# Remainders of perceptron weights made by adding transfers instead of VectorE

## The reference, cut to what matters

```python
def sq_relu_mlp(h, w_up, w_down):
    u = jax.nn.relu(h @ w_up)
    return (u * u) @ w_down
```

## Time and profile before

| what | value |
|---|---|
| runs | 1935.07, 1935.68, 1937.64 us |
| span of the profiled execution, which is also its own time as far as the profile shows | 1937.4 us |
| TensorE busy (share of the span) | 1912.2 us (99%) |
| VectorE busy | 1333.0 us (69%) |
| ScalarE busy | 837.4 us (43%) |
| GpSimd busy | 121.1 us (6%) |
| DMA | 182.62 MB, mean 94 GB/s |
| granted TensorE clock, mean | 0.998 |

### The profile page before, as it was taken

One profiled execution on the slowest core, in us unless ns is written; L12 is line 12 of the kernel. 1 busy time (PEld: TensorE's weight loads), 2 busy tenths in 40 slices (PEclk: granted clock), 3 DMA queues, 4 the chain that ended last, 5 costly groups with the idle time before them and its releaser, 6 DMA issues.

```text
span 1937.4 us, 32713 instructions
## 1 busy us (share of the span) xinstructions
PE 1912.2 (99%) x14002; PEld 1646.6 (85%) x14002; DVE 1333.0 (69%) x1755; ACT 837.4 (43%) x1254; POOL 121.1 (6%) x130
## 2 busy tenths in 40 slices
PE   8999999999999999999999999999999999999998
PEld 6877898888788898887989889889987788898897
DVE  5576869576677777767545687767677768777665
ACT  4333744344354344344224443434444645344342
POOL 1055100000000000010000000000002300000000
PEclk9999999999999999999999999999999999999999
DMA  8221402237123233224220233323342113233231
GB/s 271 88 66 66 137 10 80 88 132 128 46 89 108 87 110 109 88 78 140 90 87 23 66 98 98 109 87 109 102 144 88 50 47 106 90 106 109 87 109 44
DMA packets 138831, 182.62 MB, mean 94 GB/s; under 512 B 4917, under 2 KB 103429, under 8 KB 138304
## 3 DMA queue, kind: packets, MB, share of 16 engines
q1 hardware_dynamic: 135392, 168.91, 26.9%
q0 software_dynamic: 3296, 11.63, 2.9%
HBM read 172.66 MB, written 7.34 MB: 93 GB/s over the span
## 4 chain that ended last, share of the span: by engine, by line
PE 94%; DVE 3%; ACT 1%; issue 1%; DMA 0%; SPq 0%; DVEq 0%; ACTq 0%
PE X L1597 20%; PE M L1509 19%; PE M L1510 19%; PE M L1511 19%; PE X L643 3%; PE M L1570 1%; PE M L1571 1%; PE M L1572 1%; PE M L1925 1%; PE X L1902 1%; PE X L1913 1%; PE X L1780 1%; PE X L1749 1%; DMA raw<-in_w_in_dram 0%; PE X L1511 0%
## 5 line engine op out<-in xcount | busy, mean ns | idle before, releaser
L1510 PE MATMUL M<-u,raw_lo 128*128 128x512 f32 x728 | 287.9, 396 | 0.0
L1509 PE MATMUL M<-u,w_hi 128*128 128x512 f32 x728 | 287.9, 395 | 0.0
L1511 PE MATMUL M<-u,w_hi 128*128 128x512 f32 x728 | 286.1, 393 | 0.0
L2021 ACT ACTIVATE w_hi<-raw 128x2048 fp32r<-128x2048 f32 x113 | 215.6, 1908 | 93.5 <-PE M L1511 47.9
L2076 ACT ACTIVATE us<-X 128x256 f32<-128x256 f32 x156 | 60.2, 386 | 426.9 <-PE X L1597 426.9
L2549 DVE TENSOR_TENSOR h<-h,M 128x512 f32<-128x512 f32 x184 | 123.7, 685 | 144.7 <-PE M L1511 144.6
L1597 PE MATMUL X<-t,w_hi 128*128 128x256 f32 x936 | 173.2, 282 | 0.0
L1511 PEld LDWEIGHTS M<-u,w_hi 128*128 128x128 f32 x728 | 137.6, 189 | 32.8
L1509 PEld LDWEIGHTS M<-u,w_hi 128*128 128x128 f32 x728 | 136.8, 188 | 30.8
L1510 PEld LDWEIGHTS M<-u,raw_lo 128*128 128x128 f32 x728 | 136.7, 188 | 29.8
L2399 DVE TENSOR_TENSOR raw_lo<-raw,w_hi 128x2048 fp32r<-128x2048 f32 x57 | 130.3, 2287 | 23.7 <-ACT w_hi L2021 23.7
(11 more groups left out here) (525 smaller groups left out, 4542.2 us busy)
## 6 DMA issues: line engine op xcount, KB each, us to landing
raw<-in_w_up_dram SPq DMA_DIRECT2D x48, 1024.0 KB, 5.4
raw<-in_w_down_dram SPq DMA_DIRECT2D x48, 1024.0 KB, 5.0
raw<-in_w_in_dram SPq DMA_DIRECT2D x12, 1024.0 KB, 8.6
raw<-in_a_w_in_dram SPq DMA_DIRECT2D x12, 1024.0 KB, 5.3
h<-in_x_dram SPq DMA_DIRECT2D x16, 256.0 KB, 4.8
raw<-in_w_mk_dram SPq DMA_DIRECT2D x4, 1024.0 KB, 4.9
raw<-in_w_mv_dram SPq DMA_DIRECT2D x4, 1024.0 KB, 5.2
raw<-in_w_out_dram SPq DMA_DIRECT2D x4, 1024.0 KB, 5.1
```

The costliest lines, as they stand in the source:

```text
L1509: mm(dst, wh, xh, start=start, stop=False)
L1510: mm(dst, wl, xh, start=False, stop=False)
L1511: return mm(dst, wh, xl, start=False, stop=stop)
L2021: nc.scalar.activation(hi_of(n)[:, :, :], raw[:, n % 4], ACT.Copy).then_inc(S["w_hi_ready"], 1)
```

## The change

For the 48 down blocks and for quarters 1 to 3 of the 39 seven-product blocks, the remainder is made in two steps. ScalarE writes -hi over the raw weights (`raw_lo` <- -1.0 * `raw`, rounded to fp32r): in `hi` right behind the rounding of a down block, and in `quarters_neg` behind the fourth group of a seven-product block. Then GpSimd issues transfers with `accum_op=ALU.add` that read the same weights from DRAM again and add them to `raw_lo`, so that w - hi stands there: one transfer of 1 MB (4 rows of 2 KB in each of 128 partitions) for a down block, two for the quarters (4 rows of 512 bytes in each partition, then 4 rows of 1 KB). VectorE no longer does `lo` of down blocks nor `group_lo` 0 and 1; it goes on making the remainders of the sums. TensorE waits for all transfers of a block before its first matmul (`rest_ready`). GpSimd issues a block's transfers only when the block two earlier in this list has been taken up by TensorE: its first product, or its first finished chunk of a down block. Blocks U0 to U2 and all stages outside the perceptrons stay as they were. Some semaphores are merged to make room (`ld_tables`, `bias_step`).

```diff
@@ TensorE @@
+            def rest_ready(n):
+                wait(f"rest_lo{REST[n] % 2}", REST_DONE[n])
+
             def block_ready(n):
-                pe.wait_ge(S["w_lo_ready"], STD_NO[n] + 1)
+                if n in DOWN:
+                    rest_ready(n)
+                else:
+                    wait("w_lo_ready", LO_NO[n] + 1)
...
-                weights_ready(1)
+                rest_ready(n)
...
                 product(n, "P1", nth)
-                weights_ready(2)
                 product(n, "P2", nth)
-                weights_ready(3)
+                weights_ready(1)
...
-                weights_ready(4)
+                weights_ready(2)
@@ GpSimd: called for each perceptron @@
+            def remainders(first):
+
+                up, down = mlps[first]
+                for n in range(first, first + 32):
+                    if n not in REST:
+                        continue
+                    k, (_, _, _, g, b) = REST[n], MLP_AT[n]
+                    pool.wait_ge(S["rest_neg"], k + 1)
+                    if k >= 2:
+                        before = REST_AT[k - 2]
+                        if before in DOWN:
+                            pool.wait_ge(S["acc_done"], DONE[before] + 1)
+                        else:
+                            pool.wait_ge(S["st_mm"], 7 * FAST[before] + PRODUCT_NO["P1"])
+                    if n in DOWN:
+                        pool.dma_start(wide(raw_lo[:, n % 4]), down[:, 4 * g:4 * g + 4, 512 * b:512 * b + 512],
+                                       accum_op=ALU.add).then_inc(S[f"rest_lo{k % 2}"], 16)
+                    else:
+                        c, to_ = 512 * g + BW * b, quarters(raw_lo, n)
+                        w = up.rearrange("p (m j) n -> p m j n", j=2)
+                        pool.dma_start(to_[:, :, P:2 * P], w[:, :, 0, c + P:c + BW],
+                                       accum_op=ALU.add).then_inc(S[f"rest_lo{k % 2}"], 16)
+                        pool.dma_start(to_[:, :, BW:2 * BW], w[:, :, 1, c:c + BW],
+                                       accum_op=ALU.add).then_inc(S[f"rest_lo{k % 2}"], 16)
@@ ScalarE @@
+                if n in DOWN:
+                    nc.scalar.activation(raw_lo[:, n % 4], raw[:, n % 4], ACT.Copy, scale=-1.0).then_inc(S["rest_neg"], 1)
...
+            def quarters_neg(n):
+
+                act.wait_ge(S["st_sum"], 3 * FAST[n] + 3)
+                act.wait_ge(S["st_hi"], 4 * FAST[n] + 2)
+                x_, l_ = quarters(raw, n), quarters(raw_lo, n)
+                nc.scalar.activation(l_[:, :, P:4 * P], x_[:, :, P:4 * P], ACT.Copy, scale=-1.0).then_inc(S["rest_neg"], 1)
@@ VectorE, steady loop @@
                 for i in range(4, 30, 2):
                     add(i - 1, 3)
-                    lo(n + i + 1)
                     if i < 28:
                         sums(i + 2)
-                        group_lo(n + i + 2, 0)
-                        group_lo(n + i + 2, 1)
                     up_even(n + i)
                     up_odd(n + i)
```

More of the change, by code:

```diff
@@ L112 @@
 FAST, STD_NO, MLP_AT, HI_FREE = {}, [], {}, []
+DOWN, LO_NO, REST = {}, [], {}
 def mlp_order(last):
@@ L141 @@
                 continue
+            if _kind == "D":
+                DOWN[_n] = len(DOWN)
             _chunks = 4 if _kind == "D" else 2
@@ L156 @@
 STD_NO.append(N_END - len(FAST))
+LO_NO.append(STD_NO[-1] - len(DOWN))
+REST_AT = sorted([*DOWN, *FAST])
+REST_DONE, _count = {}, [0, 0]
+for _k, _n in enumerate(REST_AT):
+    REST[_n] = _k
+    _count[_k % 2] += 16 if _n in DOWN else 32
+    REST_DONE[_n] = _count[_k % 2]
 PRODUCTS = dict(P1=(4, 0, 3), P2=(6, 1, 0), P6=(2, 5, 3), P5=(1, 3, 2), P7=(0, 4, 3), P4=(5, 6, 1), P3=(3, 2, 2))
@@ L609, in rwkv_pe @@
                 if st == "zw":
-                    wait("ld_lora", 48)
+                    wait("ld_tables", 48)
                     wait("rw_lora", 1)
@@ L988, in gla_pe @@
             wait("acc_evac", ACC[N_GQK])
-            wait("ld_gk", 64)
+            wait("ld_tables", 160)
             wait("fold_step", 5)
@@ L1457, in _ @@
             pool.wait_ge(S["norm_ss"], 2)
[L1458 to L1461, removed]
+            pool.dma_start(onehot[:], A["onehot"]).then_inc(S["ld_tables"], 16)
+            pool.dma_start(relx[0:32, :], A["rel_table_2"]).then_inc(S["ld_tables"], 16)
+            pool.dma_start(relx[32:33, :], A["consts"][0:1, CONST["ones"][0]:CONST["ones"][0] + 16]).then_inc(S["ld_tables"], 16)
+            pool.wait_ge(S["bias_step"], 2)
             pool.dma_start(bias_rows, biasrow[:].unsqueeze(1).to_broadcast([16, P, 384])).then_inc(S["st_bias"], 16)
             pool.wait_ge(S["st_bias"], 16)
+            remainders(N_MLP1)
             for c in range(1, KT):
@@ L1606, in weights_ready @@
                 def weights_ready(k):
-                    wait("st_lo", 4 * j + k)
-                weights_ready(1)
+                    wait("st_lo", 2 * j + k)
+                rest_ready(n)
                 if j % 13 == 0:
@@ L1817, in mem_transposes @@
                 else:
-                    wait("bias_ev", 1)
+                    wait("bias_step", 2)
                 for t in range(2):
@@ L1845, in _ @@
             mem_scores(1)
-            wait("ld_rel", 48)
-            mm(X[3][0:16, 0:384], relx[:], onehot[:], start=True, stop=True).then_inc(S["bias_mm"], 1)
+            wait("ld_tables", 96)
+            mm(X[3][0:16, 0:384], relx[:], onehot[:], start=True, stop=True).then_inc(S["bias_step"], 1)
             chunk(N_MQ + 2, 1, x2_hi, x2_lo)
@@ L2619, in mlp @@
                 add(29, 3)
-                lo(n + 31)
                 final(30)
```

29 lines of the change are left out of this document (14 added, 15 removed).

## The result

The changed kernel took 1991.8 us (median of four runs, 1986.2 to 1993.9) against 1936.7 of the kernel before beside it (1935.1 to 1938.6): ratio 1.0283, 95% interval 1.0266 to 1.0299. Slower was right and the time is inside the range, but the forecast was 1957.0: it had 21 of the 55 us. The profiled execution is the quickest of the four; its span is 1984.3 us, 46.9 more than before.

A forecast was written before the change was run, and what follows sets the result against it. TensorE, busy 1912.2 of 1937.4 us, was taken as the bound; three starts 18.6, last up blocks 0.5 and tail 2.2 summed to 21.3 us, giving 1957.0 us on the median of 1935.68; range 1945 to 2050.

The forecast's parts named there:

- What bounds the kernel, and VectorE's relief at 0: Whole kernel: TensorE bounds it; it did not wait for VectorE's 4.1 us in a pair, so 0 gained.
- Rival C: Steady pairs: without VectorE's reads and writes products come closer, steps 2% shorter, 1932.6 us; chance 0.04.
- ScalarE's side in a pair at 0: Steady pairs: added negating copies of 1.90 and 1.46 us leave 3.4 us spare before the next snapshot, cost 0.
- What an adding transfer takes: All adding transfers: counted as twice the bytes, 7.7 us for a down block and 7.0 for the quarters.
- Steady pairs at 0: Steady pairs: quarters have 8.7 us for 7.0, 1.7 spare; DMA engines at 88%; cost 0.
- rival B: Steady pairs: DMA engines or transfer latency become the bound; 2088 us at three times the bytes; chance 0.28.
- Starts, 6.2 each: Start of each perceptron: TensorE stands 5.85 us for the first down block; 6.2 us each, 18.6 for three.
- rival A: All adding transfers: as quick as plain ones; starts 4.3 us each, tail nothing, 1949.1 us; chance 0.13.
- Last up block, 0.15 each: Last up block of each perceptron: a negation delays the second snapshot; 0.15 us each, 0.5 in all.
- Tail, 2.2: Kernel's end: the very last down block lands at 1908.9, first use at 1906.73; 2.2 us.
- Rival D: Starts: unseen slack and transfers landing within 2 us make no difference, 1936 us; chance 0.03.

The follow-up runs named there:

- e5: Changed kernel with the quarters negated earlier, about 4.5 us in each steady pair, same work and transfers: 1972.8 us.
- e2: Changed kernel with the quarters' remainders made by VectorE as before, only the down blocks by adding transfers: 1972.8 us.
- e8: Changed kernel, quarters negated early, VectorE making each perceptron's first two down blocks, first seven-product block and last two down blocks: 1936.0 us.
- e1: Changed kernel with transfers that overwrite instead of adding, so it computes something else: 1955.9 us.
- e7: Changed kernel with nine float32 matmuls of constants, read by nobody, ahead of the wait for each perceptron's first down block: 1980.3 us.
- e10: The changed kernel itself measured again, nothing altered: 1988.2 us, five runs from 1984.1 to 1994.2.

## Why the prediction was right or wrong, step by step

- **What bounds the kernel, and VectorE's relief at 0:** right. Pairs without a late transfer are 254.0 us for twelve with VectorE busy for 11.0 instead of 15.2 us of a pair. Rival C, that products come closer, is out: e5, e2 and e8 have the relief, or most of it, and the old step.
- **ScalarE's side in a pair at 0:** right. 1.90 and 1.48 us for the negations (1.90 and 1.46 worked out), and e5 and e8 have pairs of the old length.
- **What an adding transfer takes:** the first step that failed, and the term of the sum that was mis-sized. 7.7 us was taken for a down block, from the end of its negation to its use, and 7.0 for the quarters. At D3 it is 10.2. The runs show what the 2.5 between are. Some 0.6 is the time from the negation to the issue, which the sum put at nothing. Some 0.8 is the transfer by itself: 8.5 us from issue to landing in the tail with nothing beside it. Some 1.1 is SyncE's load, issued 1.45 us behind it: with it the landing takes 9.6. The plain part was right: 5.2 was taken, and e1's transfer in the same rows takes 5.3 alone and 5.4 in the median beside SyncE's loads. It was the adding that was priced too low: 2.5 us were taken, the price of a plain MB in rows of 8 KB, and it costs 3.1 alone and 4.1 in the median (5.4 to 9.5). Doubling the bytes was right as to the part of a row that goes with them (38 to 76 ns for a KB), but 8-KB rows were the wrong row to take it from: 1 MB is 2.5 us of each engine in such rows (8 x 309 ns) and 5.7 in rows of 2 KB that are added (32 x 178 ns), 3.2 more. The Trainium skill, Collectives: The Full Stack, section "Why ReduceScatter is half of AllGather", puts the price on the second source read; the trace agrees as far as bytes go, with 394 against 202 GB/s in the same rows, 1.95 beside the 1.93 that it has from collectives.
- **Steady pairs at 0 "with little to spare":** failed by the same number. 8.7 us was there, 7.0 was taken, 8.9 is what it is in the median. The 1.7 of margin went into that error, and what followed is neither rival B's bound by the engines (e5 gets everything back with the same bytes, at shares up to 0.96) nor nothing, but small waits in more than half of the pairs: 13 us. That the sum landed so near the edge is chance: with a landing 1 us later or earlier the term would be some 36 us larger or nearly nothing (an estimate: 36 pairs, 1 us each, and no wait over 1.4).
- **Starts, 6.2 each:** the wait for D3 was right as a mechanism, the size was not: 9.4 to 10.2. The quarters, which the sum had landing 0.35 us later still, are no term: they land while D3 runs. Of the whole 7.8 are the wait (5.85 worked out) and 1.9 are the clock at half speed behind the wait. The second is a term that was missing. e7 takes it away. With a transfer as quick as a plain one, rival A's 4.3 each, e1 has 5.8 to 6.6, again by the clock.
- **Last up block, 0.15 each:** 0.5. The snapshot was late as worked out (the negation ends 5.8 us after the block begins), and the trace lists 0.17 us of idle time for it, near the 0.15. But the products there follow each other by 0.45 and then 0.20 us, where they do by 0.12 otherwise, which makes 0.4.
- **Tail, 2.2:** 5.6. Of the 3.4 more, 1.1 are the landing (8.8 from negation to use, not 7.7) and some 1.8 the clock behind the wait.
- **Rival D, no difference:** out.

Of the 28 us between forecast and the profiled sum (49.7 - 21.3), 13.1 are the steady pairs, 10.9 the starts, 1.0 the snapshots and 3.4 the tail. By kind, some 7 are the clock and nearly all the rest are landings. That the time still lies inside the range is luck: the range reached so far up for rival B, a bound by the engines, which did not come. The median of its four runs lies 5.6 above the profiled one, the quickest; e10's profile, 7.8 us longer in its span, has 3.6 of them in the steady pairs, 2.2 ahead of the first perceptron, and the rest in starts and tail. Open stays how two transfers on different queues share the engines: it is read here as 1.1 us at D3 and 2.9 in e5, and no run isolates it.

## What to carry to other kernels

A transfer that takes over an engine's work must be compared with the time from its release to its first use, at each place apart: steady pairs, the start, the end. Where that margin is under the uncertainty of the transfer's time, assume no margin; and look for an earlier release first (here 4.9 us earlier in one engine's order gave 36 pairs back, though the landing itself came to lie only 1.7 us ahead of its use). Take the price of a transfer from one with rows of the same length. Count the low clock behind a long stall of TensorE (here 1.4 to 2.6 us behind 3.8 to 11 us), and do not add two stalls when the second transfer can land during the first. Work taken from an engine that nobody waits for is worth nothing, even 172 us of it.

## What the runs showed that I had not expected

- After 3.8 to 11 us without work TensorE's granted clock is 0.50 to 0.64 over the next 4 us (the lower level, 1.2 GHz, for most of the stretch), which cost 1.4 to 2.6 us for each block. It came in every kernel with such a wait, e1's 4.2 us included (D3 12.6, 12.6 and 13.5 us long), and not with the matmuls of constants in place of the wait. The Trainium skill, TensorE: Matmul & The Clock Gate, section "Part 1: The HAM clock gate (the "warmup" mystery)", has the engine at half clock when it comes out of idleness; the trace agrees, with 0.51 at 565.50.
- An adding transfer from DRAM into SBUF in rows of 2 KB moves 202 GB/s with all 16 engines busy and nothing beside it, a plain one in the same rows 394. The plain load of a down block, which had taken 5.0 us, takes 7.7 with adding transfers beside it (5.0 in e1, with plain ones).
- An adding issue keeps GpSimd 1.28 us, or 1.84 for 4 rows of 1 KB in each partition, where the plain one of the same shape takes 0.74 and 0.75 (e1).
- A stall can hide another: D3's late landing covered that of U4, and each alone costs as much as both.
